# One walk over w_up above 128 tokens, its gathers moved, and eight chunks of silu(c) x ada_w on GpSimd

## The reference, cut to what matters

```python
mod = silu(c) @ ada_w + ada_b                      # 1024 x 6144, six vectors of 1024
shift1, scale1, gate1, shift2, scale2, gate2 = split(mod, 6)
h = rms_norm(x, norm_mix_pre) * (1 + scale1) + shift1
y = hybrid_mixer(h, ...)                           # two kinds of attention, then merged @ w_out
x = x + gate1 * rms_norm(y, norm_mix_post)
h = rms_norm(x, norm_ffn_pre) * (1 + scale2) + shift2
y = moe_ffn(h, ...)                                # per expert: (h[toks] @ w_up[e] + b_up), clamped SwiGLU,
x = x + gate2 * rms_norm(y, norm_ffn_post)         #   @ w_down[e] + b_down, times the router's weight
```

## Time and profile before

| | us |
|---|---|
| median of 3 runs | 1415.9 |
| lowest, highest | 1414.14, 1426.24 |
| the profiled execution | 1425.02 |
| its span, first to last instruction | 1423.1 |

### The profile page before, as it was taken

The page is one execution under the profiler, slowest core; times in us unless marked ns, Lnnn a source line. Parts: engine busy times, 40 slices in busy tenths (PEclk is TensorE's granted clock), DMA queues, the critical chain, the costliest instruction groups (busy, mean ns, idle before and its releaser), DMA issues.

```text
span 1423.1 us, 21025 instructions
## 1 busy us (share of the span) xinstructions
PE 1215.5 (85%) x8163; PEld 593.7 (42%) x8164; DVE 261.3 (18%) x735; ACT 260.0 (18%) x385; POOL 0.2 (0%) x4
## 2 busy tenths in 40 slices
PE   5999899998978799998678777867788889998896
PEld 2745688645324234334233432323333333534322
DVE  1123311215112111122112111111111112120203
ACT  3035422123112102112111111111112111100211
POOL 0000000000000000000000000000000000000000
PEclk9999999996999999999999889988899999899998
DMA  9943223496469999999999999999999999854790
GB/s 337 378 163 118 89 66 112 164 347 258 184 229 420 420 416 417 418 364 420 419 419 416 418 417 419 417 417 416 418 419 417 420 415 417 356 207 149 299 408 33
DMA packets 102075, 463.83 MB, mean 326 GB/s; under 512 B 8090, under 2 KB 9330, under 8 KB 69138
## 3 DMA queue, kind: packets, MB, share of 16 engines
q1 hardware_dynamic: 100368, 461.52, 81.0%
q10 hardware_dynamic: 1666, 1.72, 0.4%
HBM read 462.16 MB, written 1.05 MB: 325 GB/s over the span
## 4 chain that ended last, share of the span: by engine, by line
PE 59%; DMA 20%; SPq 13%; issue 3%; DVE 3%; ACT 1%; DVEq 0%
PE psum L519 17%; PE psum L857 16%; DMA ring<-in_w_up 14%; PE psum L935 10%; SPq L479 7%; PE psum L806 6%; SPq L474 6%; DMA ring<-in_w_down 4%; PE psum L849 2%; PE psum L951 2%; DMA ring<-in_ada_w 1%; PE psum L525 1%; DVE area L1494 1%; PE psum L559 1%; PE psum L899 1%
## 5 line engine op out<-in xcount | busy, mean ns | idle before, releaser
L857 PE MATMUL psum<-ring,area 128*32 128x512 f32 (+3 forms) x2496 | 415.5, 637 | 78.2 <-DMA ring<-in_w_up 78.2
L857 PEld LDWEIGHTS psum<-ring,area 128*32 128x32 f32 (+2 forms) x2496 | 102.7, 122 | 378.7 <-issue 229.2
L935 PE MATMUL psum<-ring,area 128*32 128x256 f32 (+1 forms) x2080 | 201.2, 424 | 25.0 <-DVE area L1486 15.5
L806 PEld LDWEIGHTS psum<-area 128*128 128x128 f32 x1056 | 131.4, 206 | 36.0 <-issue 36.0
L806 PE MATMUL psum<-area 128*128 128x128 f32 x1056 | 138.1, 292 | 0.0
L935 PEld LDWEIGHTS psum<-ring,area 128*32 128x32 f32 (+1 forms) x2080 | 72.7, 115 | 143.4 <-issue 81.4
L1461 DVE TENSOR_SCALAR area<-psum 128x256 f32<-128x256 f32 (+1 forms) x52 | 21.8, 419 | 457.6 <-PE psum L857 457.3
L1125 ACT ACTIVATE area<-area 128x256 f32<-128x256 f32 (+1 forms) x52 | 21.4, 412 | 453.0 <-DVE area L1461 453.0
L1117 ACT ACT_TABLE_LOAD x32 | 41.1, 1283 | 301.5 <-PE psum L832 301.5
L519 PE MATMUL psum<-hT,ring 128*128 128x256 f32 x370 | 81.9, 381 | 0.0
L519 PE MATMUL psum<-ring,hT 128*128 128x512 f32 (+1 forms) x192 | 77.8, 560 | 0.0
(11 more groups left out here) (170 smaller groups left out, 658.6 us busy)
## 6 DMA issues: line engine op xcount, KB each, us to landing
ring<-in_w_up SPq DMA_DIRECT2D x256, 1024.0 KB, 19.3
ring<-in_w_down SPq DMA_DIRECT2D x128, 1024.0 KB, 22.7
ring<-in_ada_w SPq DMA_DIRECT2D x12, 2048.0 KB, 12.1
ring<-in_w_in SPq DMA_DIRECT2D x11, 2048.0 KB, 20.6
ring<-in_w_out SPq DMA_DIRECT2D x2, 2048.0 KB, 9.6
ring<-in_w_branch_b SPq DMA_DIRECT2D x1, 2048.0 KB, 7.4
cst<-in_cst ACTq DMA_DIRECT2D x1, 1168.0 KB, 8.6
x_res<-in_x SPq DMA_DIRECT2D x1, 1024.0 KB, 5.2
```

The source lines that it names most:

```text
L806: ins = pe.matmul(ps[banks[i]][:, kk % 4 * P:(kk % 4 + 1) * P], h2[:, tt, kk * P:(kk + 1) * P], S[:, tt, 0:P], start=(tt == 0), stop=(tt = ...
L857: ins = pe.matmul(ps[b][g * P // G:(g + 1) * P // G, 0:w], XT[:, kk, t0:t0 + P // G], wt[:, c0:c0 + w], start=False, stop=kk == KT - 1, sk ...
L935: ins = pe.matmul(ps[b][g * M:(g + 1) * M, 0:w], hidT[:, p, q * P + of * M:q * P + (of + 1) * M], down_weights(kk)[:, g * W + d * CW:g * W ...
```

## The change

1. **Classes 4 to 6 walk `w_up` once.** The units of the second pass use PSUM banks 3, 2, 1, 0. The running output in these banks is first copied by ACT to SBUF (`kept`; one bank for class 4, two for 5, four for 6) and copied back by DVE before L951. The extra gathers go into one bank with one ACT copy (two for class 6). The next expert's gathers move from the body's end to before the walk over `w_down`.
2. **ada4 to ada11 on POOL.** For each chunk POOL multiplies eight blocks 128x512 by a column of silu(c), and adds them up: `tensor_scalar` and `tensor_tensor`, each waited for before the next. PE turns the sums into columns of mod by one-column matmuls with ones (ada6 to ada9), and spreads gate 1 and gate 2 (ada4, ada5 and ada10, ada11) by a matmul with ones. The bias row comes by a DMA of POOL, the gains as rows over all partitions by two DMAs of ACT, and DVE multiplies them in (`gate_rows`).
3. **Order.** ada4 and ada5 move in the ring between the qk chunks, ada6 to ada9 behind the gate chunks. The spreads of gate 1 and the columns stand ahead of the branch projections. y is done as y00, y01, y10, y11 with nothing between. The transposes h2T are done by token half.

```diff
-HALVES = [1, 1, 1, 1, 2, 2, 2]
+SPILLED = [0, 0, 0, 0, 1, 2, 4]
-GATHER_BANKS = [(5, 7), (6, 7), (7, 6), (5, 7), (4, 5), (4, 5), (4, 5)]
-EXTRA_BANKS = (4, 5, 6, 4)
+GATHER_BANKS = [(5, 7), (6, 7), (7, 6), (5, 7), (7, 3), (7, 3), (3, 2)]
+EXTRA_BANKS = [[], [], [], [], [4], [4], [4, 5]]
...
+    banks = [4, 5, 6, 7, 3, 2, 1, 0]
+    for p, (G, _) in enumerate(PASSES[k]):
+        each = 2 * F // G
...
+        for m in range(3):
+            if m < 2:
+                add_ada(4 + m)
+            add_in(f"qk{m}", m * CW)
...
+            add_in(f"gate{m}", GA + m * CW)
+            add_ada(6 + m)
...
+            pe.wait_ge(ada_sum, 2)
+            spread("grow1a", grow, 0)
+            spread("grow1b", grow, 1)
+            pe.wait_ge(ada_sum, 6)
+            un.wait_free(pe, "ada_b")
+            for m in range(6, 10):
+                for q in range(4):
+                    c = 4 * (m - 6) + q
+                    ins = pe.matmul(bank("ada_b")[:, c:c + 1], ada_sums[m - 4][:, q * P:(q + 1) * P],
+                                    cst[:, C_ONE:C_ONE + 1], start=True, stop=True, skip_group_check=True)
...
-            y_unit(0, 0)
-            y_unit(1, 0)
-            ada_part("ada_b", range(4, 10), grow)
...
-            y_unit(0, 1)
-            spread("grow1a", 1, diag1, 0)
-            spread("grow1b", 1, diag1, 1)
-            y_unit(1, 1)
-            ada_part("ada_c", range(10, 12), row2)
+            for tt in range(TT):
+                for dh in range(2):
+                    y_unit(tt, dh)
+            for tt in range(TT):
+                pe.wait_ge(x1n_ready, tt + 1)
...
+            pe.wait_ge(ada_sum, 8)
+            spread("grow2a", row2, 0)
+            spread("grow2b", row2, 1)
...
+                for i in range(len(EXTRA_BANKS[k])):
+                    extras(k, i)
...
+                for u in sorted(range(n_u), key=lambda u: (units[u][1] < 4, units[u][1] in EXTRA_BANKS[k])):
+                    up_bias(u)
...
                 else:
                     for i in range(n_t):
                         turn_four(i)
+                    gathers(GATHER_BANKS[k], 0)
+                    gathers(GATHER_BANKS[k], 1)
...
                 pe.wait_ge(dn_read, MAX_D * e + MAX_D)
+                if two:
+                    pe.wait_ge(restored, e + 1)
...
                 ins.then_inc(acc_done, 1)
-                if two:
-                    pe.wait_ge(s_ready, e + 2)
-                    gathers(GATHER_BANKS[k], 0)
-                    gathers(GATHER_BANKS[k], 1)
...
+                if SPILLED[k]:
+                    act.wait_ge(acc_done, e + 1)
+                    for j in range(SPILLED[k]):
+                        ins = act.activation(kept[:, j, :], ps[3 - j], ACT.Copy)
+                    ins.then_inc(spilled, 1)
...
+                if SPILLED[k]:
+                    v.wait_ge(xg_read, 2 * e + 4)
+                    v.wait_ge(spilled, e + 1)
+                for j in range(SPILLED[k]):
+                    ins = v.tensor_copy(ps[3 - j], kept[:, j, :])
...
+            def gate_rows(n, gain):
+                v.wait_ge(ld_gain[n - 1], 16)
+                for dh, unit in enumerate((f"grow{n}a", f"grow{n}b")):
+                    un.wait_full(v, unit)
+                    ins = v.tensor_tensor(grow[:, dh * CW:(dh + 1) * CW], ps[un.bank(unit)],
+                                          gain[:, dh * CW:(dh + 1) * CW], ALU.mult)
...
+            def sum_of(m, first):
+                g = where[f"ada{m}"]
+                pool.wait_ge(slot_full[g % RING], 16 * (g // RING + 1))
+                w, to = chunk(g), ada_sums[m - 4]
+                for k in range(KT):
+                    if k == 0 and first:
+                        link(pool.tensor_scalar(to, w[:, 0, :], small[:, 0:1], None, ALU.mult))
+                    else:
+                        link(pool.tensor_scalar(w[:, k, :], w[:, k, :], small[:, k:k + 1], None, ALU.mult))
+                        link(pool.tensor_tensor(to, to, w[:, k, :], ALU.add))
+                pool.sem_inc(ada_sum, 1)
+            def gates_of(n, rows_, m):
+                pool.memset(rows_, 0.0).then_inc(sum_zero, 1)
+                pool.wait_ge(sum_zero, n)
+                pool.dma_start(rows_[0:1, :], a["ada_b"][0:1, m * CW:m * CW + D]).then_inc(ld_bias, 16)
+                pool.wait_ge(ld_bias, 16 * n)
+                sum_of(m, False)
+                sum_of(m + 1, False)
+            pool.wait_ge(silu_ready, 1)
+            un.wait_full(pool, "ada_a")
+            gates_of(1, grow[:, :], 4)
+            un.wait_full(pool, "qkT5")
+            for m in range(6, 10):
+                sum_of(m, True)
+            un.wait_full(pool, "dlo1")
+            gates_of(2, row2, 10)
```

More of the change, by code:

```diff
@@ L74, in up_units @@
     out = []
[L75 to L83 removed]
+    banks = [4, 5, 6, 7, 3, 2, 1, 0]
+    for p, (G, _) in enumerate(PASSES[k]):
+        each = 2 * F // G
+        w = min(CW, each)
+        for j in range(each // w):
+            out.append((p, banks[len(out)], w, [g * each + j * CW for g in range(G)], j * CW // 2))
     return out
 def down_tiles(k, p):
[L89 to L97 removed]
+    each = KT // PASSES[k][p][0]
+    return [(i % each, i // each) for i in range(FT)]
 C_ID = 0
@@ L335, in layer_kernel @@
         add_chunk("wo0", a["w_out"][0][:, 0:CW])
-        for m in range(4, 10):
-            add_chunk(f"ada{m}", ada[:, m * CW:(m + 1) * CW])
         add_chunk("wo1", a["w_out"][0][:, CW:D])
-        for m in range(10, 12):
-            add_chunk(f"ada{m}", ada[:, m * CW:(m + 1) * CW])
+        for m in (10, 11):
+            add_ada(m)
         NF = len(front)
@@ L371, in layer_kernel @@
             un.add(f"br{m}", 2 + m % 4)
[L372 to L374 removed]
         un.add("grow1a", 6)
         un.add("grow1b", 7)
+        un.add("ada_b", 1)
         for dh in range(2):
@@ L396, in layer_kernel @@
         released = {}
-        for name, unit in [(f"ada{m}", f"ar{m}") for m in range(12)] + [("sbq", "sbq1"), ("sbk", "sbk1"),
+        for name, unit in [(f"ada{m}", f"ar{m}") for m in range(4)] + [("sbq", "sbq1"), ("sbk", "sbk1"),
                            ("sbv", "sbv1"), ("qk0", "qk01"), ("qk1", "qk11"), ("qk2", "qk21"), ("va0", "va01"),
@@ L402, in layer_kernel @@
             released[name] = (bank_full[b], n + 1)
+        for m in range(4, 12):
+            released[f"ada{m}"] = (ada_sum, m - 3)
         names = sorted(where, key=where.get)
@@ L792, in _, with extras @@
             pe.wait_ge(cls_ready, 1)
-            def gather(b, q, first, end):
-                for i in range(2):
+            def extras(k, i):
+                n, per = P // PASSES[k][1][0], KT // len(EXTRA_BANKS[k])
+                for kk in range(per):
                     for tt in range(TT):
-                        ins = pe.matmul(ps[b][:, i * T:i * T + end - first], h2[:, tt, (2 * q + i) * P:(2 * q + i + 1) * P],
-                                        S[:, tt, first:end], start=(tt == 0), stop=(tt == 1), skip_group_check=True)
-                return ins
+                        ins = pe.matmul(ps[EXTRA_BANKS[k][i]][:, kk * n:(kk + 1) * n],
+                                        h2[:, tt, (per * i + kk) * P:(per * i + kk + 1) * P],
+                                        S[:, tt, P:P + n], start=(tt == 0), stop=(tt == 1), skip_group_check=True)
+                ins.then_inc(xe_full, 1)
             def gathers(banks, i):
@@ L894, in turn_four @@
                                 lo, hi = 4 * c, min(4 * c + 4, blocks)
-                                u = max(u for u in range(n_u) if units[u][1] == p and units[u][5] < hi * P)
-                                pe.wait_ge(act_ready, acts + (n_u if two else u + 1))
+                                u = max(u for u in range(n_u) if units[u][0] == p and units[u][4] < hi * P)
+                                pe.wait_ge(act_ready, acts + u + 1)
                                 for q in range(lo, hi):
@@ L902, in turn_four @@
                             at += 1
-                if not two:
-                    pe.wait_ge(s_ready, e + 2)
-                    pe.wait_ge(gt_read, e + 1)
+                pe.wait_ge(s_ready, e + 2)
+                pe.wait_ge(gt_read, e + 1)
                 if k == 0 or k == 1:
@@ L1370, in _ @@
                 ins.then_inc(bank_free[4 + q], 1)
-            mod_part("ada_c", 40, 48)
-            diagonals(diag2, 40, 3)
             un.wait_full(v, "logit")
```

227 lines of the change are left out of this document (99 added, 128 removed).

## The result

| | before | after |
|---|---|---|
| median of 20 runs each, us | 1417.9 | 1408.7 |
| lowest | 1412.46 | 1405.85 |
| highest | 1426.24 | 2090.23 |
| the profiled execution's span | 1423.1 | 1408.1 |

The ratio is 0.9931, with a 95% interval of 0.9917 to 0.9945: 9.2 us less, within 1%. The forecast was 1391, and its range ended at 1406. One run of after was slow, 2090.23 us at a mean granted clock of 0.707, and is not in the interval; the next highest took 1410.47. The profiled execution of before lay 7 above this median, so the spans differ by more, 15.0.

A forecast was written before the change was run, and what follows sets the result against it. PE's path before the weights' stream, and in the dip at the expert above 128 tokens, was taken to count: 16.8 + 8.1 = 24.9 off 1425.0 gives 1400.1, the median 9.1 lower, 1391. Own range 1385 to 1397; with rivals 1382 to 1406.

The forecast's parts named there:

- POOL's price: Front, ada6 to ada9 on POOL: twice DVE's times, some 72 us, done at 246 before PE waits at 253.7.
- Rival (a): Front: POOL is late, a factor above 2.2; 1405 at 2.6, 1398 at 2.4; chance 0.13.
- 8 us of room: Front: POOL's ada9 is done at 246, in time by 8 before PE's wait at 253.7.
- The front: PE's path to the first expert: gain 16.8, with y from 279.7 and the first walk near 349.
- Behind y: From y's end to hT's end: 11.7 in place of 14.8, as the first half's norm runs under y; gain 3.1.
- (d): Rival: parts deliver half, by lower clock after PE's idle or extra biases at 0.50; 1395 to 1400; chance 0.08.
- The big body: The one expert above 128 tokens: gain 8.1 from one walk over w_up and the moved gathers.
- the biases: Big body, all five units at once: 4.4 at full clock; with the lower level until 1234.1, the walk starts at 1235.9.
- The walk: Big body, one walk over w_up: 34.9, ending at 1270.8 where it ended at 1276.3; gain 5.5.
- The move of the gathers: Big body, gathers ahead of the down walk: gap 1.8 more, 3.84 at the end and 0.6 of copy go; net 2.6.
- Rival (c): Idle of 7.5 behind the big expert depends on code place: shorter 1385, chance 0.08; another elsewhere 1398, chance 0.04.
- Rival (b): DVE and POOL block each other in four slots, past 2.9 of cover: PE loses 39, ending at 1430; chance 0.05.

The follow-up runs named there:

- the products mended: GpSimd's products written as tensor_tensor with the column broadcast, in place of tensor_scalar, against the changed kernel: 1397.5 us, 0.9864 of the kernel before.
- the columns moved as well: The changed kernel with both edits, PE's columns behind y and GpSimd's products as tensor_tensor: 1390.4 us, 0.9795 of the kernel before.
- increments: 192 semaphore increments on PE early in the program, added to the kernel before with only the first part of the change: 1428.5 us, 1.0062.
- the kernel before again: The kernel before, unchanged, taken once more for a second profile: 1417.2 us in one run.
- part 1 alone: The kernel before with only the single walk over w_up, its bank copies and the moved gathers: 1414.0 us, 0.9976; again on another chip 1413.3 us, 0.9960.
- late columns: The changed kernel with PE's wait for ada9 and the 32 column matmuls moved behind y: 1393.6 us, 0.9838 of the kernel before.

## Why the prediction was wrong

**The step that failed is POOL's price.** The prediction took twice VectorE's times for both kinds of instruction, 72 us for ada6 to ada9, and put the point where PE begins to wait at a factor of 2.2. Measured were 92.0 us against VectorE's 34.7: a factor of 2.65 with the gaps between instructions (about 0.1 each, where I had 0.04), and of 2.5 without. The sum was guessed near enough, 1.27 against 0.69, a factor of 1.84. The product was not: 1.56 to 1.59 against 0.48, 3.3 times. The Trainium skill's factor of 1.96 (GPSIMD Engine Reference, section Performance versus the Vector engine) is for a sum, and there the trace comes near it with 1.84; I carried it over to another kind of instruction, whose row lay nowhere in the trace.

**What hung on it.** Rival (a) is what happened, at its upper end: I had "at 2.6 PE stands 14 and the result is 1405", and PE stood 12.4 at 2.65. The forecast rested on 8 us of room. I gave (a) 0.13 although its price had no row at all and its point of decision lay only a tenth above the value that I had chosen; a value picked between open ends deserves no such trust. And the rival was priced at the wait alone. The wait also took the clock, 3.4 in the columns, a quarter more. The branch group behind the columns lost 1.9, which no term of the sum had, wait or no wait. These 5.3 carried it out of the range. Two of the recorded sums are off as well, without deciding anything: at 2.6 the prediction's own terms (173.9 + 2.6 x 34.7 + 2.4 = 266.5) make PE stand 12.8 and not 14, and the chances listed for faster by more than 1% add up to 0.885, not 0.85.

**The front without that.** With the products mended, y began at 280.4 (forecast 279.7) and the first walk at 346.5, with the columns moved as well at 344.9 (forecast 349). The first walk of the old front, without increments, starts at 359.7, 361.7, 362.6 and 366.2 in four profiles. I had read the slowest of the four: its stretch behind y was 45.1, and 39.3 to 39.5 in the three others, the same work at another clock. From their mean of 362.6 the gain is 16.1 and 17.6, forecast 16.8; the changed kernel's 364.1 is a loss of 1.5. These are rows of the kernel before again, and of before, for one and the same matmuls:

```profile
345.77 3.71 PE L785 MATMUL psum<-b_down_sb,area 32*128 32x256 f32 x16 [0.72 <-ACT area L992]
```

```profile
347.00 7.19 PE L785 MATMUL psum<-b_down_sb,area 32*128 32x256 f32 x16 [0.51 <-ACT area L992]
```

**Behind y** I had 3.1 of gain from the norms that now run under y. From y's end to the first walk it is 37.5 in after (326.6 to 364.1), against 39.4: 1.9. Part of what the order gives goes back in the clock, as (d) said: the last eight transposes take 1.97 behind an idle of 6.60, where the eight before took 1.04.

**The big body.** Forecast 8.1. From the extra gathers to the last work of the body it was 90.7 and 88.4 in the two profiles of before, and is 81.6 in after and 81.1 with part 1 alone: 6.8 to 9.6. Inside, the biases took 6.7, about the 6.9 that I had with the low clock in it. The walk took 36.75 and not 34.9, and not by the clock: the table of windows has 1.00 for all of it in after (1239.7 to 1276.3), and it is 36.75 in all eleven profiles of one walk, with or without an idle at the entry. So 1.9 of the 5.5 for the walk was a mis-sized term. The down walk took 19.84, where it had been 22.45 with a granted clock of 0.50 from 1281.3 to 1286.0, which I hadn't counted. The move of the gathers was worth 0.9, not 2.6. These are errors of both signs, and that the sum fits is luck.

**Rival (c)** came in part: the idle did move with the code, to the entry and at nearly the same size. I had kept 7.5 of it, which is about what the kernel still pays. What I had not seen is that its place has a price: about 3.5.

**Rival (b)**, contention of DVE and POOL, is real and hidden. Three rows of the first slot's chain of DVE in after (timeline of DVE):

```profile
179.08 0.81 DVE L1318 TENSOR_SCALAR small<-small 128x2 f32<-128x2 f32 x1
...
181.84 1.25 DVE L1322 TENSOR_SCALAR area<-area,small 128x384 f32<-128x384 f32 x1
183.02 1.06 DVE L1323 TENSOR_SCALAR area<-area,small 128x768 f32<-128x768 f32 x1
```

They took 0.17, 0.42 and 0.61 before [the last: rows 5]; all three read and write SBUF alone, where the prediction counted two. The chain takes 7.2 (176.87 to 184.08) instead of 5.3 (175.57 to 180.84): 1.9 more, inside the 2.9 of cover. The last slot ends no later: the instruction behind it starts at 252.7 with late columns, at 251.7 to 254.8 in the four profiles without POOL's work. In the branch products of after, one instruction with an input from PSUM, and one with both from SBUF:

```profile
284.14 0.42 DVE L1331 TENSOR_TENSOR area<-psum,area 128x256 f32<-128x256 f32 x1 [0.80 <-PE psum L525]
...
284.93 1.48 DVE L1335 TENSOR_TENSOR area<-area 128x256 f32<-128x256 f32 x1
```

All eight of the first kind took 0.42, and the eight of the second 0.42 to 1.48. That agrees with the Trainium skill (SBUF — State Buffer, section Who interferes with whom), by which a VectorE instruction with two SBUF inputs meets GpSimd's reads and one with at most one SBUF input does not, unless it runs in a two-port mode. It counts `tensor_scalar` among those that can, which fits the three rows above; no run here shows the mode.

**The sum as it came.** Front -1.5 (forecast 16.8), body with idle and tail 199.4 to 189.9, 9.5 (forecast 8.1): together 8.0, against 9.2 in the medians. With both edits of the columns and the products: 17.6 + 9.0 = 26.6, against 27.0.

## What to carry to other kernels

Price an instruction on an engine where it has never run by its own kind, and if no row gives it, keep a deadline that hangs on it away from the critical path: placed behind y, in a stretch in which PE waited anyway, the columns cost nothing that can be seen and made the slow engine harmless. The wait of PE of 12.4 us was paid twice, in itself and in the columns behind it at half the clock, here 3.4 or a quarter on top. Before reading a few microseconds as an edit's worth, take a second profile of the kernel before, and look whether an idle without a releaser has only changed its place.

## What the runs showed of the hardware

- A product 128x512 with a scalar for each partition took 1.59 us on GpSimd in the mean (`tensor_scalar`, after), and as `tensor_tensor` with the column broadcast 1.06 (the run with cheaper products). A sum of two full tensors took 1.27 and 1.29. On VectorE a sum took 0.69 and a 128x768 product 0.61 (before).
- An instruction that only increments a semaphore took 0.15 us on PE, in the stretch in which 96 stood in a row.
- An idle of 7 to 10 us behind a branch on PE came and went with 18 instructions at the program's start, worth 10 us between the medians of 1390.4 and 1400.5. Instruction transfers of 16 KB stood inside the long idles of all profiles.
- The same front took 39.3 to 45.1 us from y's end to the first expert in four profiles. In the slowest the output's bias took 7.19 at a granted clock of 0.50, in the profile taken again 3.71 at 1.00.
